# Keeping the residual in SBUF through an expert stage, with 18 staging slots instead of 20, and storing the expert rows from ScalarE

## What is computed

```python
x = x + gate1 * rms_norm(hybrid_mixer(h), g_post_mix)     # the residual
h = rms_norm(x, g_pre_ffn) * (1.0 + scale2) + shift2
logits = h @ router_w + router_b                          # 32 experts
top_v, top_i = lax.top_k(logits, 4)
...
gu = xb @ w_gate_up[e] + b_gate_up[e]                     # per block of tokens of expert e
act = x_glu * sigmoid(1.702 * x_glu) * (x_lin + 1.0)
y = act @ w_down[e] + b_down[e]
...
x = x + gate2 * rms_norm(weighted sum of the four y of a token, g_post_ffn)
# then the second block: h = rmsnorm(x), z = h @ w_in_2, ...
```

## Time and profile before

| | |
|---|---|
| median of 3 runs | 1888.09 us (1885.24 to 1890.99) |
| the profiled execution | 1888.09 us, span of its trace 1886.5 us |
| granted TensorE clock, mean over the span | 0.935 of full |
| TensorE, matmuls busy | 1660.4 us (88%) |
| VectorE busy | 1144.8 us (61%) |
| ScalarE busy | 852.8 us (45%) |
| GpSimd busy | 338.3 us (18%) |
| moved by DMA | 520.80 MB, mean 276 GB/s |
| expert stage | from about 367 to 1475 us of the span |

### The profile page before, as it was taken

The page is one execution under the profiler, slowest core; times in us unless marked ns, Lnnn a source line. Parts: engine busy times, 40 slices in busy tenths (PEclk is TensorE's granted clock), DMA queues, the critical chain, the costliest instruction groups (busy, mean ns, idle before and its releaser), DMA issues. The chain is left out here.

```text
span 1886.5 us, 50543 instructions
## 1 busy us (share of the span) xinstructions
PE 1660.4 (88%) x16925; PEld 878.5 (47%) x16926; DVE 1144.8 (61%) x1698; ACT 852.8 (45%) x1131; POOL 338.3 (18%) x467
## 2 busy tenths in 40 slices
PE   6999889688899899989978899899886369998897
PEld 3999655333344344334422344233231146877753
DVE  5795444665677677657745577566553274973664
ACT  5334532064456566546634466465443144533411
POOL 0000000022223232222211233222120300530000
PEclk9999999788999999989988999999887679999999
DMA  9871673268969999993899989998999732211101
GB/s 333 274 253 63 183 212 126 95 269 346 426 270 397 424 424 408 424 425 131 355 425 426 425 345 421 424 425 355 424 425 397 263 86 75 79 56 48 54 7 45
DMA packets 136452, 520.80 MB, mean 276 GB/s; under 512 B 20131, under 2 KB 58804, under 8 KB 87093
## 3 DMA queue, kind: packets, MB, share of 16 engines
q1 hardware_dynamic: 117988, 487.81, 65.1%
q0 software_dynamic: 18240, 31.46, 4.6%
q10 hardware_dynamic: 146, 0.48, 0.1%
HBM read 494.67 MB, written 24.91 MB: 275 GB/s over the span
## 5 line engine op out<-in xcount | busy, mean ns | idle before, releaser
L1880 DVE COPY ring<-staging 128x1536 f32 (+1 forms) x638 | 598.6, 962 | 315.8 <-PE banks L1755 137.5
L1813 ACT ACTIVATE ring<-staging 128x1536 f32 (+1 forms) x319 | 472.6, 1486 | 496.8 <-PE banks L1755 247.6
L1755 PE MATMUL banks<-staging,rowsT 128*32 (+1 forms) x1268 | 608.1, 625 | 93.7 <-ACT ring L1813 55.4
L1755 PE MATMUL banks<-ring,rowsT 128*32 128x512 f32 x3840 | 617.6, 626 | 0.0
L1755 PEld LDWEIGHTS banks<-staging,rowsT 128*32 128x32 f32 x1268 | 128.8, 112 | 501.6 <-issue 496.2
L1778 PE MATMUL banks<-ring,hiddenT 128*32 128x256 f32 x3840 | 306.6, 394 | 0.0
L1778 PE MATMUL banks<-staging,hiddenT 128*32 x1280 | 305.6, 394 | 0.8 <-ACT hiddenT L1824 0.5
L1778 PEld LDWEIGHTS banks<-staging,hiddenT 128*32 128x32 f32 x1280 | 145.7, 114 | 165.3 <-issue 67.6
L1778 PEld LDWEIGHTS banks<-ring,hiddenT 128*32 128x32 f32 x3840 | 161.8, 114 | 0.0
L602 PE MATMUL banks<-w_in_hi,hT 128*128 128x256 f32 (+1 forms) x768 | 147.3, 291 | 1.3 <-issue 1.3
L1755 PEld LDWEIGHTS banks<-ring,rowsT 128*32 128x32 f32 x3840 | 145.1, 112 | 0.0
(11 more groups left out here) (437 smaller groups left out, 1963.0 us busy)
## 6 DMA issues: line engine op xcount, KB each, us to landing
staging<-in_w_gate_up SPq DMA_DIRECT2D x250, 1024.0 KB, 12.8
staging<-in_w_down SPq DMA_DIRECT2D x128, 1024.0 KB, 12.7
stage<-in_w_mod SPq DMA_DIRECT2D x21, 1024.0 KB, 6.0
stage<-in_w_in SPq DMA_DIRECT2D x25, 512.0 KB, 4.0
stage<-in_w_in SPq DMA_DIRECT2D x11, 1024.0 KB, 5.7
expert_rows<-rows_leaving POOLq DMA_DIRECT2D x80, 128.0 KB, 8.3
expert_rows<-catT SPq DMA_DIRECT2D x1, 7936.0 KB
early<-in_w_gate_up SPq DMA_DIRECT2D x6, 1024.0 KB, 16.0
```

Source lines behind the costliest of these rows:

```text
L1755: mm = pe.matmul(k.bank(0)[c * SLOTS:(c + 1) * SLOTS, :], rowsT[:, q % 2, row], w, start=first and q == 0, stop=not first and q == KT - 1, ...
L1813: act.activation(ring[:, pos % RING, :], staged(i, e, pos, PART, CHUNK - PART), ACT.Copy).then_inc(act_filled, 1)
L1880: dve.tensor_copy(ring[:, pos % RING, :], staged(i, e, pos, PART, CHUNK - PART)).then_inc(dve_filled, 1)
```

## The change

1. `k.x` is allocated once for the whole kernel. The tensor `x_mixed`, the four stores to it in the router, the load in `stage_second`, and the waits for them are gone. The second block adds to the same tile.
2. `STAGED` goes from 20 to 18, and so the circle of slots from 160 KB to 144 KB in each partition.
3. The tile `rows_leaving`, GpSimd's copy into it and `store_rows` are gone. ScalarE itself issues the store from `y_rows`, right behind `read_y` and ahead of `hidden_turned`; `read_y` now waits until the store of the unit before has landed. GpSimd's loop only moves and gathers rows.

```diff
-STAGED = 20
+STAGED = 18
...
 def persistent(k):
+    k.x = k.sb("x", [P, NT, D])
...
-                    sp.wait_ge(x_ready, t + 1)
-                    sp.dma_start(d["x_mixed"][t * P:(t + 1) * P, :], k.x[:, t, :]).then_inc(x_out, 16)
                     sp.wait_ge(h2_ready, t + 1)
...
-                def store_rows(n):
-                    pool.wait_ge(y_read, n + 1)
-                    after(pool, y_out, 16 * n)
-                    pool.sem_inc(y_due, 1)
-                    pool.tensor_copy(leaving[:], y[:]).then_inc(y_free, 1)
-                    pool.wait_ge(y_free, n + 2)
-                    pool.sem_inc(y_seen, 1)
-                    pool.dma_start(store_of(n * SLOTS), leaving[:]).then_inc(y_out, 16)
...
-                with pool.Fori(2, units) as i:
+                with pool.Fori(1, units) as i:
                     move_rows(i + 2)
                     gather(i + 3, landing, 0, rows_in)
-                    store_rows(i - 1)
...
                 def read_y(n, done):
                     act.wait_ge(chunk_done, done)
-                    act.wait_ge(y_free, n + 1)
+                    act.wait_ge(y_out, 16 * n + 16)
                     act.activation(y[:], k.bank(4)[:, 0:GLU], ACT.Copy).then_inc(y_read, 1)

+                def store_y(n):
+                    act.wait_ge(y_read, n + 1)
+                    act.sem_inc(y_seen, 1)
+                    act.dma_start(store_of(n * SLOTS), y[:]).then_inc(y_out, 16)
...
                     read_y(i - 1, i * CHUNKS + CHUNKS)
+                    store_y(i - 1)
                     hidden_turned(i)
...
                 read_y(end, units * CHUNKS + CHUNKS)
+                store_y(end)
+                act.wait_ge(y_out, 16 * units + 16)
...
-                sp.dma_start(k.x[:], d["x_mixed"].rearrange("(t p) n -> p t n", p=P)).then_inc(x_in, 16)
...
-        k.x = k.sb("x_back", [P, NT, D])
```

More of the change, by code:

```diff
@@ L244, in stage_front @@
     nc, d = k.nc, k.d
-    k.x = k.sb("x", [P, NT, D], at=front)
     k.gate2 = k.sb("gate2", [P, D], at=front)
@@ L1222, in stage_router @@
         gate2_out = sem("gate2_out")
-        x_out = sem("x_out")
         const_in = sem("router_const_in")
@@ L1268, in _ @@
                 sp.wait_ge(gate2_out, 16)
-                sp.wait_ge(x_out, 16 * NT)
             @block.tensor
@@ L1558, in stage_experts @@
         y = sb("y_rows", [P, D // QUARTERS])
-        leaving = sb("rows_leaving", [P, D // QUARTERS])
         gsum = sb("gsum", [P, LINE])
@@ L1589, in stage_experts @@
         y_read = sem("expert_y_read")
-        y_due = sem("expert_y_due")
-        y_free = sem("expert_y_free")
         y_seen = sem("expert_y_seen")
@@ L1708, in _ @@
                 gather(3, landing, 0, rows_in)
[L1709 to L1712, removed]
-                with pool.Fori(2, units) as i:
+                with pool.Fori(1, units) as i:
                     move_rows(i + 2)
                     gather(i + 3, landing, 0, rows_in)
-                    store_rows(i - 1)
-                end = pool.value_load(k.table[0:1, TABLE - 2:TABLE - 1], min_val=NE - 1, max_val=NBLK - 1)
-                store_rows(end)
                 pool.wait_ge(rows_in, 16 * units + 16)
-                pool.wait_ge(y_out, 16 * units)
-                pool.sem_inc(y_seen, 1)
             @block.tensor
@@ L1834, in read_y @@
                     act.wait_ge(chunk_done, done)
-                    act.wait_ge(y_free, n + 1)
+                    act.wait_ge(y_out, 16 * n + 16)
                     act.activation(y[:], k.bank(4)[:, 0:GLU], ACT.Copy).then_inc(y_read, 1)
+                def store_y(n):
+                    act.wait_ge(y_read, n + 1)
+                    act.sem_inc(y_seen, 1)
+                    act.dma_start(store_of(n * SLOTS), y[:]).then_inc(y_out, 16)
+                act.sem_inc(y_out, 16)
                 rows_turned(0, 0)
@@ L2055, in stage_second @@
         gate2_in = sem("gate2_in")
-        x_in = sem("s2_x_in")
         choice_in = [[sem(f"choice_in{t}_{half}") for half in range(2)] for t in range(NT)]
@@ L2395, in add_acc @@
                     chain(dve.reciprocal(acc_rstd[:, t:t + 1], acc_rstd[:, t:t + 1]))
-                    if t == 0:
-                        dve.wait_ge(x_in, 16)
                     dve.scalar_tensor_tensor(k.x[:, t, :], choices[t][:, 2, :], acc_rstd[:, t:t + 1],
@@ L3147 @@
     dram["expert_rows"] = nc.dram_tensor("expert_rows", [NBLK * SLOTS, D], F32, kind="Internal").ap()
-    dram["x_mixed"] = nc.dram_tensor("x_mixed", [S, D], F32, kind="Internal").ap()
     dram["gate2"] = nc.dram_tensor("gate2_row", [1, D], F32, kind="Internal").ap()
```

## The result

The changed kernel takes 1998.28 us (1993.56 to 2001.99, four runs) against 1889.54 us for the kernel before (1885.24 to 1892.97): a ratio of 1.0575, 95% interval 1.0541 to 1.0610. The sign was forecast; the size was not. The sum gave 16 us more, the chip gave 109. (One of the four executions of the half store, further down, took 5720.49 us, for a reason that no run shows, and isn't in its ratio.)

What follows compares the result with a forecast made beforehand. The expert stage was taken to alternate between DMA at its limit and pauses for free slots, six times. 1888.1 us + 31 (slots) - 4.5 (stage's end) - 10 (residual's load) = 1904.6, said as 1904; 8-in-10 range 1893 to 1915.

Steps and rivals of the forecast that it cites:

- The sum: Whole kernel: 1888.1 + 31 - 4.5 - 10 = 1904.6 us, stated as 1904.
- The 8.3 us in the earlier trace: Expert stage: landing time of a store by GpSimd's queue, taken as below the 11.51 us step, so `read_y` never waits.
- "Cost 0", the issue on ScalarE: Expert loop: issuing the store on ScalarE takes 0.50 us, delays line 1824 by 0.7 us, costs 0; upper bound 6 us.
- the argument about the 1.74 us of cover: Expert loop: ScalarE idles 1.74 us before the ring copy of chunk 5, which hides the 0.7 us delay.
- "ScalarE's cover is too small": Rival, expert loop: chunk 5's ring copy is late by 0.7 us in 60 units, 42 us more, 1946 us; chance 4%.
- The slots: 31 us: Expert stage, 18 slots for 20: two loads, 5.2 us, longer wait in each of six runs; bounds 21 and 41 us.
- the six runs: Expert stage: stretches after SyncE's six pauses, at whose ends engines wait for arriving weights; each was to lose 5.2 us.
- One of my signs: Trace of the changed kernel: SyncE's wait at the free of a slot exceeds 176.7 us by about 30.
- The residual's load: 10 us: Second block: without the residual's 2.1 MB ahead, the first weight tile lands 10 us sooner; bounds 5 and 14 us.
- The end of the stage: 4.5 us: Expert stage's end: ScalarE issues the last store 2.7 us sooner, landing 1.8 us quicker; gain 4.5 us, bounds 2.0 and 6.
- GpSimd's finishing work: Expert stage's end: part of the 6.74 us before the next stage; counted as leaving the path only in the 6 us bound.
- The other reading in the prediction: Expert stage's end: issuers share 16 DMA engines, so landing gains nil; gain 2.0 us, total 2.5 us higher.

Runs made afterwards that it cites:

- the half store: The changed kernel storing only the first 64 partitions of each unit's rows, with zeros written over the whole tensor in the mixers: 2008.82 us, ratio 1.0620.
- the flat store: The changed kernel storing each unit's 128 KB to the same place as 128 consecutive rows of 1 KB, not four columns of 32: 1890.91 us, ratio 1.0005.

## Why the prediction was wrong, step by step

**The step that failed: "`read_y` also waits for the landing of the store before; that store is 11.51 us older and lands in 8.3 us by GpSimd's queue, so it waits for nothing in the loop."** The 8.3 us in the earlier trace rows were of the same shape and size, but GpSimd's store goes in packets of 4 KB, eight on each of four engines, and ScalarE's in pieces of 1 KB, 32 on each of four engines (shown by the counts and times of the packets, and by the flat store, which differs in nothing but the destination's form and has eight pieces on each of 16). From issue to released read it is about 15 us while loads run; most steps of a busy stretch grow from 11.5 to between 15.0 and 15.6 us. Such a step also keeps slots longer, and so DMA stands still more. The other row that I had for a store on a hardware queue, 2.6 us for 512 KB, had 128 rows outermost and no loads beside it; I used it for the end of the stage only, where the store landed 2.9 us after its issue. I made no bound for a landing above 11.51 us, and so the range had no room for it. A second `y_rows` tile, so that the read needn't wait for the store just before, is a rival cure that was not tried.

**"Cost 0", the issue on ScalarE.** The price of 0.50 us from a single row was off by a factor of two: 1.07 us for this form, 0.35 us for the flat one. With the flat form the argument about the 1.74 us of cover holds, steps are 11.51 us. In the changed kernel a step where no landing is waited for is 11.9 us; there are some 20 of them. So the rival "ScalarE's cover is too small" is a small second part of the loss in the changed kernel, 0.4 us in such a step and about 8 us in all.

**The slots: 31 us, measured 29.** Right in size, and the cause in the main: in the trace with 18 slots alone the reads of the rows fall behind those of before in the six runs by 6.0, 4.7, 0.8, 4.7, 6.8 and 2.6 us, 25.6 in all, and hardly in between. So four of the six show about the 5.2 us that I gave each; my taking that none would absorb it was wrong for the third and the last. One of my signs was wrong: I had said SyncE's wait at the free would be longer by about 30 us. With slots alone it is longer by 62, with more pauses but a longest one that hardly grew:

```profile
SPq L1664 <- PE banks L1755: 238.6, 109, 50.1
```

109 waits instead of 80, yet only what is lost in the runs reaches the end.

**The residual's load: 10 us, measured 15** (1917.79 to 1902.39 us), just beyond my upper bound of 14. It is the difference of two medians whose executions spread over 8 and 14 us, so that excess isn't clear of noise. The mechanism was right. I had moved only the tile's landing by the 10 us of the residual's bytes; with those bytes gone the tile's own transfer was also quicker: 13.1 us after its stage began, against 29.5:

```profile
1501.03 1.26 SPq L2101 DMA_DIRECT2D z<-in_b_down  x3
```

```profile
1514.16 1.06 ACT L2252 ACTIVATE w_in_hi<-stage 128x1024 fp32r<-128x1024 f32 x1 [6.86 <-DMA stage<-in_w_in]
```

There the sum over the choices then waits 1.80 us for TensorE, so that 14.4 of the 16.3 us arrive.

**The end of the stage: 4.5 us, measured 5.1**, made up otherwise than I thought: the issue comes 2.6 us sooner after the last read, the store lands in 2.9 us instead of 3.9, and 1.5 us are GpSimd's finishing work, which I had in the upper bound only. The other reading in the prediction, the landing no sooner and a gain of 2.0 us, doesn't hold here.

Taken together: with a store of eight pieces on each of 16 engines the change gives no loss at all (1890.91 us), 14 us below my sum. The slots and the residual account for the way to 1902.39 us. The flat store then beats GpSimd's by 11.5 us: 6.3 are the end of the stage (3.70 us from the last read to the next stage against 9.98), 6.0 lie inside the expert stage (from first to last read 1077.9 against 1083.9 us), and what makes the 6.0 was not tried. (The two traced executions differ by 8.6 us only, so elsewhere some go the other way.)

## What to carry to other kernels

A transfer's landing time read in a profile belongs to its issuer and to its form, and not only to its size: before one is moved to another queue, ask on how many engines it will run there and in how many packets on each, since beside a full queue of loads each packet waits its turn. A wait for a landing inside a loop needs to be priced against the landing while the other queue is full. And a queue's order costs where its first item is small and awaited: moving a load behind the awaited one gave 7 to 9 us here, of the 15 us that keeping the data in SBUF gave, at no cost in buffers.

## What the runs showed of the hardware

- ScalarE's store of 128 pieces has 132 packets when its destination's outermost dimension is 4, 66 for 64 pieces and dimension 2, 144 with 128 outermost, and 48 for 32 pieces with 32 outermost. GpSimd's store with outermost 4 has 144: 32 of 4 KB, 96 of 16 B and 16 of 4 B.
- The form sets the time of the issue as well: 1.07 us with (4, 32, 256), 0.35 us with (128, 256), on the same engine for the same bytes.
- Beside the loads, whose packets of 8 KB take 0.31 us, the pieces of a store on one engine follow each other at 0.35 us (1 KB), 0.33 us (512 B) or 0.46 us (GpSimd's packets of 4 KB).
- Under full load a store takes about 15 us from issue to the released read when it has 32 pieces of 1 KB on each engine, be it four engines or two; with eight pieces on each of 16 it lands in 6.8 us. Fewer loads in flight (8.0 us to a load's landing for 13.3) didn't shorten it.
